# Expert gates of a product-key layer: one-hot products per token replaced by indirect DMAs that add into a zeroed table

## The reference, cut to what matters

```python
v1, i1 = lax.top_k(s1, P_TOPK)
v2, i2 = lax.top_k(s2, P_TOPK)
cand = (v1[..., :, None] + v2[..., None, :]).reshape(t, P_HEADS, P_TOPK * P_TOPK)
best, pos = lax.top_k(cand, P_TOPK)
expert = (jnp.take_along_axis(i1, pos // P_TOPK, axis=-1) * N_KEYS
          + jnp.take_along_axis(i2, pos % P_TOPK, axis=-1))
gate = jax.nn.softmax(best, axis=-1)
...
hid = jax.nn.gelu(jnp.einsum('pd,phkd->phk', xb, u_tab[eb]), approximate=False)
return jnp.einsum('phk,phkd->pd', (gb * hid).astype(xb.dtype), v_tab[eb])
```

## Time and profile before

| | before |
|---|---|
| median of 3 runs | 3211.19 us (3210.83 to 3211.24) |
| profiled execution, first to last instruction | 3209.0 us |
| PE busy | 3191.6 us, 99% |
| DVE busy | 2030.1 us, 63% |
| ACT busy | 1447.3 us, 45% |
| POOL busy | 496.9 us, 15% |
| memory traffic | 644 MB, 201 GB/s |

### The profile page before, as it was taken

How to read it: one execution, slowest core, us unless ns; L and a number is a source line. 1 busy time by engine, 2 the same in 40 slices (tenths; PEclk the granted TensorE clock), 3 DMA queues, 4 the chain that set the end, 5 groups by cost and what they waited for, 6 DMA issues and landing times.

```text
span 3209.0 us, 48201 instructions
## 1 busy us (share of the span) xinstructions
PE 3191.6 (99%) x19975; PEld 2854.0 (89%) x19975; DVE 2030.1 (63%) x1837; ACT 1447.3 (45%) x1271; POOL 496.9 (15%) x418
## 2 busy tenths in 40 slices
PE   9999999999999999999999999999999999999999
PEld 7888899999999888888989999999999888888887
DVE  5455665556555667765476888999975555555554
ACT  5454453333433364464444444555544433334333
POOL 0000000000000002136200002888840000000000
PEclk9999999999999999999999999999999999999999
DMA  7444565555555453342255566677676656556563
GB/s 282 165 159 158 172 225 194 196 186 193 195 187 193 158 183 119 132 158 105 93 211 204 199 216 222 224 251 251 229 263 259 241 225 261 228 230 257 226 261 118
DMA packets 129572, 644.18 MB, mean 201 GB/s; under 512 B 12672, under 2 KB 45840, under 8 KB 60304
## 3 DMA queue, kind: packets, MB, share of 16 engines
q1 hardware_dynamic: 95792, 623.03, 53.3%
q10 hardware_dynamic: 33632, 18.99, 1.9%
HBM read 606.31 MB, written 35.66 MB: 200 GB/s over the span
## 4 chain that ended last, share of the span: by engine, by line
PE 97%; DVE 1%; ACT 1%; DMA 0%; SPq 0%; issue 0%; DVEq 0%; ACTq 0%
PE pj L305 12%; PE pj L304 12%; PE pj L306 12%; PE pj L282 7%; PE pj L281 7%; PE pj L280 7%; PE pj L1774 4%; PE pj L1772 4%; PE pj L890 4%; PE pj L892 4%; PE pj L1773 4%; PE pj L891 4%; PE pm L282 2%; PE pt L282 2%; PE pt L281 2%; PE pm L281 2%
## 5 line engine op out<-in xcount | busy, mean ns | idle before, releaser
L262 ACT ACTIVATE hi<-raw 128x2048 fp32r<-128x2048 f32 x534 | 1023.8, 1917 | 1372.7 <-PE pj L306 640.7
L269 DVE TENSOR_TENSOR lo<-raw,hi 128x2048 fp32r<-128x2048 f32 x400 | 918.5, 2296 | 677.5 <-ACT hi L262 676.7
L304 PE MATMUL pj<-xh,hi 128*128 128x256 f32 x3328 | 919.9, 276 | 0.0
L305 PE MATMUL pj<-xl,hi 128*128 128x256 f32 x3328 | 918.8, 276 | 0.0
L306 PE MATMUL pj<-xh,lo 128*128 128x256 f32 x3328 | 918.8, 276 | 0.0
L305 PEld LDWEIGHTS pj<-xl,hi 128*128 128x128 f32 x3328 | 625.0, 188 | 0.6
L304 PEld LDWEIGHTS pj<-xh,hi 128*128 128x128 f32 x3328 | 624.8, 188 | 0.6
L306 PEld LDWEIGHTS pj<-xh,lo 128*128 128x128 f32 x3328 | 624.8, 188 | 0.0
L269 DVE TENSOR_TENSOR lo_in<-raw,hi 128x2048 fp32r<-128x2048 f32 x134 | 308.1, 2300 | 268.9 <-ACT hi L262 268.4
L2495 POOL TENSOR_SCALAR hotA<-cst,slotT 128x128 fp32r<-128x128 f32 x256 | 337.9, 1335 | 462.0 <-ACT slotT L2333 425.4
L1772 PE MATMUL pj<-hi,xh 128*128 128x512 f32 x576 | 232.3, 403 | 0.0
(11 more groups left out here) (408 smaller groups left out, 4243.8 us busy)
## 6 DMA issues: line engine op xcount, KB each, us to landing
raw<-w_peer SPq DMA_DIRECT2D x256, 1024.0 KB, 6.3
raw<-w_mlp SPq DMA_DIRECT2D x128, 1024.0 KB, 4.8
raw<-w_in SPq DMA_DIRECT2D x102, 1024.0 KB, 4.8
raw<-w_out SPq DMA_DIRECT2D x32, 1024.0 KB, 4.8
raw<-w_q SPq DMA_DIRECT2D x16, 1024.0 KB, 4.9
act_scratch<-hidU SPq DMA_DIRECT2D x32, 512.0 KB, 3.0
gates_scratch<-stage ACTq DMA_DIRECT2D x8, 2048.0 KB, 17.5
hidV<-act_scratch SPq DMA_DIRECT2D x32, 512.0 KB, 3.7
```

What stands on the lines that cost most here:

```text
L262: nc.scalar.activation(hi[:, j, :], raw[:, j, :], ACT.Copy).then_inc(hi_ready, 1)
L269: nc.vector.tensor_tensor(low(q)[:, j, :], raw[:, j, :], hi[:, j, :].bitcast(F32), ALU.subtract).then_inc(lo_ready, 1)
L304: nc.tensor.matmul(o, hi[:, j, cols], xh[:, k0 + k, :], start=clears, stop=False, skip_group_check=True)
L305: nc.tensor.matmul(o, hi[:, j, cols], xl[:, k0 + k, :], start=False, stop=False, skip_group_check=True)
```

## The change

The table in memory is laid out [expert row, block, expert x token], filled with zeros in the first half of the MLP, and the 32768 gates (256 tokens x 8 heads x 16) are added into it by 256 indirect DMAs that POOL issues, one for each of 2 x 128 tokens, 8 heads and 16 picks: 128 gates of 4 bytes each. The one-hots, the gate matmuls, the copies out of PSUM and the table's writes are gone. The router does all its steps for one pair of heads before the next pair (14 steps to a pair), so that the first pair's places are known early, and computes the place of each gate in the table. The up blocks 12 to 29 become a loop of two blocks. The diff, cut to its core:

```diff
+        def zero_pool(pool):
+            pool.wait_ge(pe_used, Q_MLP * SLOTS)
+            nc.gpsimd.memset(zeros[:, :], 0.0).then_inc(g_zero, 1)
+            pool.wait_ge(g_zero, 1)
+            for s in range(PEER_SB):
+                pool.wait_ge(pe_used, (Q_MLP + s // 2) * SLOTS + 2 * (s % 2) + 1)
+                pool.dma_start(gates_d[:, s, :], zeros[:, :]).then_inc(g_zeroed, 16)
+
+        def scatter_pool(pool):
+            pool.wait_ge(g_zeroed, 16 * PEER_SB)
+            cells = gates_d.rearrange("p s (n a) -> (p s n) a", a=1)
+            for h in range(H):
+                for t in range(TT):
+                    pool.wait_ge(g_share, h // 2 + 1)
+                    pool.wait_ge(g_placed, 2 * (h // 2) + t + 1)
+                    if h >= 1:
+                        pool.wait_ge(g_added[t], 16 * TOPK * h)
+                    for j in range(h * TOPK, (h + 1) * TOPK):
+                        pool.indirect_dma_start(cells, bass.IndirectOffsetOnAxis(place[:, t, j:j + 1], 0), res[:, 0, t, j:j + 1], None,
+                                                compute_op=ALU.add).then_inc(g_added[t], 16)
...
@@ block2_act
                     act.wait_ge(nm_pair, 1)
+                    act.wait_ge(g_zeroed, 16 * PEER_SB)
                     evacuate(0, 0)
...
@@ the router, a pair of heads b at a time
+        def select(dve, n, b, t, s_):
+            link(dve, dve_link, n, nc.vector.tensor_tensor(
+                oh[:, :, :], pqf[:, s_, t, picks(b)].unsqueeze(2).broadcast_to([P, 2 * TOPK, TOPK]),
+                cst[:, C_IOTA, 0:TOPK].unsqueeze(1).broadcast_to([P, 2 * TOPK, TOPK]), ALU.is_equal))
...
+        def gate_places(dve, n, b, t):
+            flat = pqf[:, 0, t, picks(b)]
+            link(dve, dve_link, n, nc.vector.scalar_tensor_tensor(flat, res[:, 1, t, picks(b)], float(NK), res[:, 2, t, picks(b)], ALU.mult, ALU.add))
+            nc.vector.tensor_scalar(place[:, t, picks(b)], flat, float(TT * P), small[:, S_TOK + t:S_TOK + t + 1], ALU.mult, ALU.add).then_inc(g_placed, 1)
 
         def router_dve(dve, n, k):
 
+            b, step = k // 14, k % 14
...
+            elif step == 8:
+                gate_parts(dve, n, b)
+            elif step == 9:
+                gate_shares(dve, n, b)
+            else:
+                t, s_ = (step - 10) // 2, step % 2
+                select(dve, n, b, t, s_)
+                if s_ == 1:
+                    gate_places(dve, n, b, t)
...
@@ u_turns
-            for s in range(U_GATES):
+            for s in range(U_ROUTER):
                 block(s, s % 2)
-
-            for i in range(GROUPS // 16):
-                for m in range(4):
-                    block(i * 4 + (U_GATES + m), m % 2, i, 4 * m)
-            for s in range(U_AFTER, PEER_SB):
+            with eng.Fori(U_ROUTER // 2, PEER_SB // 2 - 1) as i:
+                block(i * 2, 0)
+                block(i * 2 + 1, 1)
+            for s in range(PEER_SB - 2, PEER_SB):
                 block(s, s % 2)
...
@@ peer_pe
-                    if is_block(s, U_GATES - 1) and j == 2:
-                        slots()
-                    if i is not None:
-                        gate_group(16 * i + g0 + j)
...
@@ peer_act, up_block: the gate copies and writes go, one Exp for each pair of heads
-                    if 0 <= u < GROUPS:
-                        first_share(u)
-                    if u % 8 == 0 and 8 <= u <= GROUPS:
-                        write_gates(u - 1)
+                    k = 9 + 4 * s + j
+                    if isinstance(s, int) and s < U_ROUTER and k % 14 == 9:
+                        act.wait_ge(r_exp, 2 * (k // 14) + 1)
+                        nc.scalar.activation(res[:, 0, :, picks(k // 14)], res[:, 0, :, picks(k // 14)], ACT.Exp).then_inc(r_exp, 1)
...
@@ peer_dve, up_block
-                    if 0 <= u < GROUPS:
-                        hot_group(n, u)
...
-                    if 0 < u <= GROUPS:
-                        sum_group(u - 1)
...
@@ peer_sp, up_quad
                     if j == 0 and is_block(s, PEER_SB - 2):
-                        for half in range(2):
-                            sp.wait_ge(g_wr[half], 16 * (GROUPS // 16))
+                        for t in range(TT):
+                            sp.wait_ge(g_added[t], 16 * TOPK * H)
...
@@ block.gpsimd
             att1_pool(pool)
+            zero_pool(pool)
             hgrn_pool(pool)
             squares_pool(pool)
             delta_pool(pool)
-            hot_pool(pool)
+            scatter_pool(pool)
```

More of the change, by code:

```diff
@@ new lines, in gate, with gate_parts @@
+        def gate(b):
+            return res[:, 0, :, picks(b)].rearrange("p t (h j) -> p t h j", j=TOPK)
+        def gate_parts(dve, n, b):
+            dve.wait_ge(tk, (b + 1) * TK_GROUP)
+            b_ = best[:, :, heads(b), :]
+            for t in range(TT):
+                ins = nc.vector.tensor_tensor(gate(b)[:, t, :, :], b_[:, t, :, :], b_[:, t, :, 0:1].broadcast_to([P, 2, TOPK]), ALU.subtract)
+            ins.then_inc(r_exp, 1)
+            pos_ = pos[:, :, heads(b), :].rearrange("p t h j -> p t (h j)")
+            nc.vector.tensor_scalar(pq[:, 0, :, picks(b)], pos_, 4, None, ALU.logical_shift_right)
+            nc.vector.tensor_copy(idxf[:, :, 4 * b:4 * b + 4, :], idx[:, :, 4 * b:4 * b + 4, :])
+            link(dve, dve_link, n, nc.vector.tensor_scalar(pq[:, 1, :, picks(b)], pos_, 15, None, ALU.bitwise_and))
+            for s_ in range(2):
+                ins = nc.vector.tensor_copy(pqf[:, s_, :, picks(b)], pq[:, s_, :, picks(b)])
+            link(dve, dve_link, n, ins)
@@ L2268, in peer_pe, with up_block @@
         def peer_pe(pe):
-            def slots():
-                pe.wait_ge(r_sel, 5)
-                pe.wait_ge(r_sc, 4)
-                for q_ in range(3):
-                    for t in range(TT):
-                        tr = nc.tensor.transpose(pm[:, q_ // 2, (q_ % 2) * 256 + t * P:(q_ % 2) * 256 + t * P + P], res[:, q_, t, :], ident)
-                tr.then_inc(r_slotT, 1)
-            def gate_group(n):
-                pe.wait_ge(r_slot, 1)
-                if n >= 2:
-                    pe.wait_ge(r_gc, n - 1)
-                pe.wait_ge(r_A, n + 1)
-                pe.wait_ge(r_B, n + 1)
-                for a in range(4):
-                    c0 = (a % 2) * 2 * NK
-                    mm = nc.tensor.matmul(g_pair[n % 2][:, a // 2, c0:c0 + 2 * NK], hotA[n % 2][:, a, :],
-                                          hotG[n % 2][:, a, :, :].rearrange("p s b -> p (s b)"), start=True, stop=True)
-                mm.then_inc(r_G, 1)
-            def up_block(s, par, i=None, g0=0):
+            def up_block(s, par):
                 if is_block(s, 0) or is_block(s, 1):
@@ L2306, in down_block @@
                 for n in range(4):
-                    if first and n == 0:
-                        pe.wait_ge(r_gc, GROUPS)
                     if first and n >= 2:
```

183 lines of the change are left out of this document (49 added, 134 removed).

## The result

The change makes the kernel **slower: 3400.4 us** (median of 4 runs, 3399.1 to 3409.9) against 3211.1 us before, a ratio of 1.060 [1.058, 1.061]. I had forecast 3181.5 us, in a range up to 3300. Sign and range are both wrong.

A forecast was written before the change was run, and what follows sets the result against it. PE's instructions end to end, 99% busy, were taken as the bound. Span 3209.0 - 29.7 = 3179.3 us, all other terms 0, plus 2.2 around it: 3181.5 us, 0.93% faster; range 3177 to 3300, forecast chance 0.70.

The forecast's parts named there:

- the price of one indirect DMA: POOL's scatter in the up blocks: 1.335 us each, hotA's mean, so 256 end at 2132 us, 280 us early.
- the right limit: Scatter in the up blocks: 2.44 us per DMA on average, (2414 - 1790) / 256, before PE stalls at slot 120.
- Rival A: Scatter late at SP's wait, up block 30: at 2.9 us a DMA 118 us late, 3299.5 us; chance 0.22.
- the most: hotA's longest time as price of a scatter DMA: 3.491 us, ending at 2684 us, 270 us late.
- My reason against a dear DMA: Against the late scatter in the up blocks: DVE is lighter there than where hotA was measured; no size given.
- PE's spacing stays 0.1133: Up blocks: up matmuls still start 0.1133 us apart, a slot of 48 taking 5.44 us.
- What PE loses: Expert layer: 256 gate matmuls, 29.0 us, and six transposes, 0.67 us, leave PE; together 29.7 us, all on the path.
- DVE, ACT and the zeroing: Up blocks: some 15 us more DVE work, 9 us more ACT; MLP: 32 zeroing DMAs of 512 KB; cost 0.
- Rival B: Up blocks: scatter packets crowd out chunk loads; at 0.20 us a packet 160 us more, 3344 us; chance 0.05.
- Rival C: Expert layer: gate matmuls only filled PE's waits for chunks, removal yields nothing, 3211 us; chance 0.03 together with small stalls.

The follow-up runs named there:

- half the scatter: Changed kernel with only heads 0 to 3 added (128 of 256 indirect DMAs): 3210.4 us; the same with qT0 and tiles behind it moved up 384 bytes: 3180.9 us.
- the copies' run: Changed kernel with plain copies in place of all 256 adds, queue of 1024 bytes, tiles moved up 384 bytes, doubles not summed: 3180.8 us, ratio 0.991.
- run 3632: Not a run number: 3632 counts packets in the copies' run, the changed kernel with plain copies in place of adds, 3180.8 us.

## Why the prediction was wrong, step by step

**The step that failed is the price of one indirect DMA.** The prediction worked out the right limit: 2.44 us on average, or SP, and then PE, comes to stand. The runs bear it out. A chunk's way from issue to PE, put at 10.3 us, was 11.2 in after (2641.9 - 2630.7), and with the 15.4 us found above the limit is (2424.6 - 15.4 - 1790) / 255 = 2.43, and 2.15 us a DMA were in time where 2.64 were not. Everything hung on one value, and I took 1.335 us, the mean of POOL's short operation on the same number of partitions. The measured 3.27 us is made up of the following, none of which that row holds. 1.56 us is the work of issuing a DMA of 128 cells and 0.30 the gap to the next. 0.22 us is what the splits add to the work in the mean. The other 1.19 us is waiting for places in a queue of 1024 bytes: 0.70 when alone, more beside the up blocks, as chunk loads lengthen these waits. In the stretch beside the up blocks the same shows as 1.87 us of work (157.12 / 84) in 3.57 us (300 / 84), against 1.56 in 2.59 when they have stopped. The least of hotA, 0.594 us, is not half of what any add took (1.555 at least).

**Rival A's mechanism is what happened, and its price was too low as well.** 2.9 us (the landing of the smallest write) gave 118 us; at 3.27 the same formula gives 1790 + 837 = 2627, the last start, as it must, since 3.27 is taken from it. I gave A 0.22. The row that I had named as "the most", 3.491 us, was nearer to the truth than my value, but by luck: most of the 3.27 us beyond the bare work is waiting for places, of which the prediction had no term. My reason against a dear DMA, that DVE is lighter than where hotA was measured, fails: DVE is busy only 137.44 of 300 us in after, and the adds are lengthened all the same, to 1.87 us; no row of before showed how a longer piece of POOL work meets the same splits. A short one meets them like this: the hotA that starts at 2103.78 us in before, beside the split from 2103.82, takes 2.72 us, and the two behind the split, from 2106.49, 0.60 each. That a short one slips between them more often is my reading, and was not tried.

**"PE's spacing stays 0.1133"** was taken for granted and is wrong: 0.1176 us from the first key scores on, through the tiles' addresses, in a part of the diff that I costed at nothing. It would have taken away the whole gain even with the scatter on time (half the scatter: 3210.4 against 3180.9). In after it is hidden: PE merely gets later to a point where it waits anyway.

**What PE loses** was right: 29.7 us of gate matmuls and transposes forecast. 3210.7 - 3180.8 = 29.9 us came out where nothing else is late (the copies' run, against the kernel before measured beside it).

**DVE, ACT and the zeroing** were right. An operation of a selection, estimated at 0.7 us, takes 0.68 to 0.69 in after (`oh`, 16 of each). PE's only wait over 1.3 us beside the long one is at the first chunks of the kernel, as before, and a chunk of the MLP, beside half of which the zeroing runs, lands in 4.9 us (4.8 before):

```profile
raw<-w_mlp SPq DMA_DIRECT2D x128, 1024.0 KB, 4.9
...
gates_scratch<-zeros POOLq DMA_DIRECT2D x32, 512.0 KB, 5.5
```

**Rival B, packets crowding out the chunks,** is refuted. From 2100 to 2340 us POOL's queue (packets, MB, share of 16 engines) and the chunks' landing were:

```profile
q0 software_dynamic: 9648, 0.04, 6.5%
...
raw<-w_peer SPq DMA_DIRECT2D x43, 1024.0 KB, 4.8
```

0.065 x 16 x 240 / 9648 = 0.026 us a packet. I had the threshold at 0.122 and the price at 0.20, which no run shows. An add does cost the DMA engines several times a plain write: from 2100 to 2330 us 9216 packets at 6.5% are 0.065 x 16 x 230 / 64 = 3.7 us of one engine for each of 64 adds, and in the copies' run 3632 packets at 1.1% are 0.36 us for each of 113.5 copies. Chunks land in 4.8 us, against 5.1 before. The chunks slow the scatter, not the other way, by these numbers. **Rival C** is refuted as well: PE's time does come back once nothing is late.

## What to carry to other kernels

A long row of small DMAs issued by GpSimd is to be priced by its rate, not by one operation: work to issue one (in after 1.56 us and 0.30 to the next), plus waiting for places in the descriptor queue (1.19), plus what VectorE's long operations add (0.22; these two trade, as from 1024 to 1536 bytes, where idle time fell by 0.63 us and work rose by 0.29); compare that with the time at which somebody waits for the last of them. If no row shows that rate, measure it alone first, or keep the range as wide as the ignorance; and where a sum crosses from gain to loss within the bounds of one unknown, that unknown decides the chances, not the central value. And when tiles move, count the matmuls in a fixed stretch before and after: "busy" stayed at 100% while PE did 4% less.

## What the runs showed of the hardware

- An indirect DMA of 128 single cells of 4 bytes costs POOL 1.55 us as an add and 0.96 us as a copy, and 0.30 us to the next. An add is also more packets: POOL's queue has 41472 in after (256 adds), 23040 with 128 adds, so 144 an add, and the rest of 4608 is the zeroing, 144 for each of its 32 DMAs; with 256 copies it has 12800, so 32 a copy.
- The size of the descriptor queue sets the rate of adds, alone: 2.55 us at 1024 bytes, 1.85 at 16384. In this kernel it gives 3.27 at 1024, 2.93 at 1536 and 2.64 to 2.74 at 3072, with 7, 3 and 1 long gaps to 16 adds, while the work of an add rises from 1.78 to 2.28 us.
- An add that starts 0.45 us into VectorE's two-input split of 2.29 us takes 3.27 us instead of 1.56 and ends 1.43 us behind the split; the split keeps its 2.29. Beside subtractions of 2.29 us without a pause, with a queue of 16384 bytes, an add takes 1.90 us.
- Tiles at certain addresses (those of `keys` or those of `qT` at remainder 448 by 512 instead of 320) leave all later matmuls of 256 columns 4% further apart from the first key scores on (0.1176 us instead of 0.113), at the full granted clock. Behind the idle stretch of after the spacing is 0.113 us again, and the down blocks' matmuls of 512 columns show no difference.
